# Small inputs by the GpSimd queue, a new order for the first two tiles, w_co in whole rows, and crossbar transposes for MLP tiles 1 to 3

## What is computed

```python
# sub-layer 1
u, bg, cg, h = jnp.split(xn @ w_in, [...], axis=-1)        # 512 columns each
y_pool = pool_mix(u_ext, ...)   # four groups: mean over the last 2, 4, 8, 16 rows - u, then 128x128 maps
y_conv = bg * conv3(cg * h)     # depthwise, causal, width 3
merged = concat(group_rmsnorm(y_pool, 4 groups), group_rmsnorm(y_conv, 8 groups))
x = x + rmsnorm(merged @ w_out, g_mix_post)
# sub-layer 2
x = x + rmsnorm(cross_attn(rmsnorm(x, g_x_pre), mem_k, mem_v, w_q, w_co), g_x_post)
# sub-layer 3
hid = jnp.square(jax.nn.relu(rmsnorm(x, g_ff_pre) @ w_up))  # 4096 columns
x = x + rmsnorm(hid @ w_down, g_ff_post)
```

## Time and profile before

| | |
|---|---|
| median of 3 runs | 883.66 us (882.21 to 885.01) |
| the profiled execution | 873.56 us |
| its span on the slowest core (7) | 872.0 us (cores: 859.7 to 872.0) |
| PE busy | 829.7 us, 95% |
| DVE, ACT, POOL busy | 390.7, 373.0, 102.5 us |
| chain that ended last | PE 83%, DMA 8%, DVE 3%, ACT 2%, POOL 2%, issue 2% |
| granted TensorE clock | 0.995 of full speed on core 7 |
| DMA | 100.31 MB moved, 115 GB/s over the span |

### The profile page before, as it was taken

The page is one execution under the profiler, slowest core; times in us unless marked ns, Lnnn a source line. Parts: engine busy times, 40 slices in busy tenths (PEclk is TensorE's granted clock), DMA queues, the critical chain, the costliest instruction groups (busy, mean ns, idle before and its releaser), DMA issues.

```text
span 872.0 us, 14089 instructions; the slowest of 8 cores (859.7 to 872.0 us)
## 1 busy us (share of the span) xinstructions
PE 829.7 (95%) x4818; PEld 404.9 (46%) x4818; DVE 390.7 (45%) x538; ACT 373.0 (43%) x806; POOL 102.5 (12%) x169
## 2 busy tenths in 40 slices
PE   2899999999998999999998999999999999999996
PEld 2444445554453455445454445444444444444442
DVE  4587767567865565668223213232222231322112
ACT  4557656657775565676332113340223311233101
POOL 4462102413210000100010000000000000000000
PEclk9999999999999999999999999999999999999999
DMA  8993076870069545794889724883139830185001
GB/s 206 220 167 52 18 234 168 159 109 1 2 88 161 108 153 174 130 166 94 146 144 166 174 97 103 144 151 93 49 112 159 152 85 25 49 146 96 17 33 49
DMA packets 31674, 100.31 MB, mean 115 GB/s; under 512 B 2666, under 2 KB 15978, under 8 KB 26356
## 3 DMA queue, kind: packets, MB, share of 16 engines
q0 software_dynamic: 20592, 65.15, 44.0%
q1 hardware_dynamic: 10436, 34.14, 11.6%
q10 hardware_dynamic: 576, 0.13, 0.1%
HBM read 142.28 MB, written 18.07 MB: 184 GB/s over the span
## 4 chain that ended last, share of the span: by engine, by line
PE 83%; DMA 8%; DVE 3%; ACT 2%; POOL 2%; issue 2%; SPq 0%; POOLq 0%; DVEq 0%; ACTq 0%
PE ps L639 80%; PE ps L644 3%; DMA wco<-w_co 3%; DMA wdn_131<-w_down 2%; DMA up_124<-w_up 1%; POOL sAB_94 L677 1%; DMA sT<-sconv 1%; DMA O_57<-mem 1%; POOL sAB_95 L677 1%; ACT xs_60 L668 0%; DVE xT_55 L675 0%; DVE X L688 0%; DVE O_57 L675 0%; ACT rf_101 L668 0%; DVE O_58 L675 0%
## 5 line engine op out<-in xcount | busy, mean ns | idle before, releaser
L675 DVE TENSOR_TENSOR O_57<-ps,gp 128x1024 f32<-128x1024 f32 x24 | 29.3, 1222 | 100.3 <-PE ps L639 74.3
L675 DVE TENSOR_TENSOR O_58<-ps,gp 128x1024 f32<-128x1024 f32 x24 | 29.3, 1222 | 98.2 <-PE ps L639 61.0
L668 ACT ACTIVATE rt_122<-ps 128x512 bf16<-128x512 f32 x64 | 38.2, 597 | 72.0 <-PE ps L639 69.7
L668 ACT ACTIVATE rt_121<-ps 128x512 bf16<-128x512 f32 x64 | 38.2, 596 | 71.8 <-PE ps L639 71.8
L668 ACT ACTIVATE O_58<-ps 128x1024 f32<-128x1024 f32 (+1 forms) x25 | 24.9, 996 | 98.7 <-PE ps L639 97.9
L668 ACT ACTIVATE O_57<-ps 128x1024 f32<-128x1024 f32 (+1 forms) x26 | 25.3, 972 | 97.6 <-PE ps L639 93.8
L639 PE MATMUL ps<-xT_55,win 128*128 128x512 bf16 x256 | 63.1, 392 | 1.3 <-DVE xT_55 L675 1.3
L639 PE MATMUL ps<-xT_56,win 128*128 128x512 bf16 x256 | 59.3, 379 | 0.1
L639 PE MATMUL ps<-xT_56,up_123 128*128 128x512 bf16 x192 | 42.4, 379 | 0.0
L639 PE MATMUL ps<-xT_55,up_124 128*128 128x512 bf16 x192 | 42.4, 379 | 0.0
L639 PEld LDWEIGHTS ps<-xT_55,win 128*128 128x128 bf16 x256 | 25.1, 100 | 31.1 <-issue 5.7
(11 more groups left out here) (302 smaller groups left out, 1504.2 us busy)
## 6 DMA issues: line engine op xcount, KB each, us to landing
up_123<-w_up POOLq DMA_DIRECT2D x11, 1024.0 KB, 9.2
up_124<-w_up POOLq DMA_DIRECT2D x11, 1024.0 KB, 10.4
up_125<-w_up POOLq DMA_DIRECT2D x10, 1024.0 KB, 10.2
x<-X SPq DMA_DIRECT2D x16, 512.0 KB, 4.0
X<-x SPq DMA_DIRECT2D x16, 512.0 KB, 4.3
yp<-X SPq DMA_DIRECT2D x16, 512.0 KB, 2.6
X<-xp SPq DMA_DIRECT2D x8, 512.0 KB, 6.5
win<-w_in POOLq DMA_DIRECT2D x4, 768.0 KB, 35.9
```

Of the source, the lines that this page charges most:

```text
L668: return e.activation(out=L(out), in_=L(in_), func=func, scale=scale, **kw)
L675: opts.append(("dve", lambda e, L: e.tensor_tensor(out=L(out), in0=L(in0), in1=L(in1), op=op), c_dve(n, per)))
```

## The change

Seven edits:

1. f4, Xs and sT are loaded from POOL's queue, sT first, and so are gp and gps of the first sub-layer.
2. Tile 1 is loaded by four loads of 512 KB behind w_in part 3, where one of 2 MB stood ahead of it.
3. The work of the first two tiles gets another order. Before: groups 0 to 3 of tile 0 and tile 1 interleaved, then the conv groups in pairs. After: the four pool groups of tile 0, the sample rows' states, conv groups 0 and 1 of tile 0 with the halves of tile 1's `pre_tile` behind them, the four pool groups of tile 1, its conv groups 0 and 1, and then conv groups 2 and 3 in pairs.
4. For tiles 0 and 1 the squares in `pre_sub` go to a spare buffer `junk` and no longer to xs. The scaling of rows may be done by DVE, ACT or POOL, as the planner finds, in every `pre_sub`.
5. w_co lies in memory as one row of 32 KB per partition, no longer as 16 blocks with 2 KB per partition, and is loaded with the planner's rate for large blocks.
6. For the MLP of tiles 1, 2 and 3 the transposes of xT are DMAs: `pre_tile_dma` squares and scales as before, then one `dma_start_transpose` on SP per sub-tile writes the 128x1024 block transposed into xT, and eight DVE operations apply the column gains in place.
7. For the last sub-tile of all, `post_halves` does square, multiply, add and store by halves of 512 columns.

The planner's cost for issuing a load from POOL changes as well.

```diff
-    wout_d = din("w_out", [128, 8192]); wco_d = din("w_co", [16, 128, 512])
+    wout_d = din("w_out", [128, 8192]); wco_d = din("w_co", [128, 8192])
+    junk = at("junk", A0 + 16384, D, BF16)
+    def scale_rows(out, in_, rs):
+        n = ncols(out)
+        P.add([("dve", lambda e, L: e.tensor_scalar(out=out, in0=in_, scalar1=rs, scalar2=None, op0=ALU.mult), c_dve(n, 0.5)),
+               ("act", lambda e, L: e.activation(out=out, in_=in_, func=AF.Copy, scale=rs), c_act(n)),
+               ("pool", lambda e, L: e.tensor_scalar(out=out, in0=in_, scalar1=rs, scalar2=None, op0=ALU.mult),
+                0.2 + n * 0.0009)], reads=[in_, rs], writes=[out])
-        return P.add([(q, lambda e, L: e.dma_start(out=out, in_=in_), 0.9 if q == "pool" else 0.43)],
+        return P.add([(q, lambda e, L: e.dma_start(out=out, in_=in_), 0.5 + nbytes / desc * 0.0005 if q == "pool" else 0.43)],
     def load_late():
-        load(f4[:, :], fold4[:, :], 65536)
-        load(Xs[:, :], xs4[:, :], 131072)
-        load(sT[0:32, :], spool[:, :], 65536)
-        load(sT[32:36, :], sconv[:, :], 8192)
+        load(sT[0:32, :], spool[:, :], 65536, q="pool")
+        load(sT[32:36, :], sconv[:, :], 8192, q="pool")
+        load(f4[:, :], fold4[:, :], 65536, q="pool")
+        load(Xs[:, :], xs4[:, :], 131072, q="pool")
-    def pre_sub(X, r, gc, dst):
+    def pre_sub(X, r, gc, dst, sq_out=None):
-        act(xs, X, AF.Square, accum=ss)
+        act(xs if sq_out is None else sq_out[0:r, :], X, AF.Square, accum=ss)
         rs = rstd(ss, r)
-        ts(xs, X, rs, ALU.mult)
+        scale_rows(xs, X, rs)
+    def post_halves(ps, X, gp, dst):
...
+        act(half(Ob, 0), ps.v(0, 128, 0, 512), AF.Square, accum=s0)
+        act(b0, s0, AF.Identity, scale=1.0 / D, bias=epsb[:, 0:1])
+        tt(half(Ob, 0), ps.v(0, 128, 0, 512), half(gp, 0), ALU.mult)
+        act(half(Ob, 1), ps.v(0, 128, 512, 1024), AF.Square, accum=s1)
+        tt(half(Ob, 1), ps.v(0, 128, 512, 1024), half(gp, 1), ALU.mult)
+        act(a, s1, AF.Ln, scale=1.0 / D, bias=b0)
+        act(rs, a, AF.Exp, scale=-0.5)
+        for h in range(2):
+            stt(half(X, h), half(Ob, h), rs, half(X, h), ALU.mult, ALU.add)
+            dma("sp", half(dst, h), half(X, h), 262144, wr=False)
+    def pre_tile_dma(t, gc, buf):
+        for i in range(NSUB):
...
+            act(xs, X, AF.Square, accum=ss)
+            rs = rstd(ss, 128)
+            scale_rows(xs, X, rs)
+            dst = r3(buf[:, :], 8)[:, :, i * 128:(i + 1) * 128]
+            P.add([("sp", lambda e, L, dst=dst, xs=xs: e.dma_start_transpose(out=dst, in_=xs), 0.43)],
+                  reads=[xs], writes=[dst], nbytes=262144)
+        for c in range(8):
+            v = buf[:, c * TN:(c + 1) * TN]
+            ts(v, v, gcs[:, gc * 8 + c:gc * 8 + c + 1], ALU.mult, per=0.25)
-    pre_tile(0, 0, xT[0])
-    second = load_four(1, xp, "pool")
-    for k in range(3, 7):
-        load_win(k)
+    pre_tile(0, 0, xT[0], junk)
+    load_win(3)
+    load_tile(1, xp, q="pool")
+    load_win(4)
+    load_win(5)
+    load_win(6)
...
-    load_gp("g_mix_post", second)
-    load_gps(0, second)
+    load_gp("g_mix_post", q="pool")
+    load_gps(0, q="pool")
     for g in range(4):
         step(pool_group(0, g))
-        if g == 1:
-            pre_tile(1, 0, xT[1])
-        if g >= 2:
-            step(pool_group(1, g - 2))
-    for g in range(2, 4):
+    ext_states()
+    ext_pool_rest()
+    ext_conv(0)
+    step(conv_group(0, 0))
+    pre_tile(1, 0, xT[1], junk, (0, 2))
+    ext_conv(1)
+    step(conv_group(0, 1))
+    pre_tile(1, 0, xT[1], junk, (2, 4))
+    for g in range(4):
         step(pool_group(1, g))
-    ext_pool_rest()
-    for cc in range(4):
+    for cc in range(2):
+        step(conv_group(1, cc))
+    for cc in range(2, 4):
         ext_conv(cc)
         step(conv_group(0, cc))
         step(conv_group(1, cc))
-            wload(wco[:, :], wco_d, 0, 16)
+            load(wco[:, :], wco_d[:, :], 4194304, q="pool", desc=16384)
-            pre_tile(t + 1, 2, xT[(t + 1) % 2])
+            pre_tile_dma(t + 1, 2, xT[(t + 1) % 2])
```

More of the change, by code:

```diff
@@ L795, in post @@
         return stt(X, Ob, rs, X, ALU.mult, ALU.add)
+    def post_halves(ps, X, gp, dst):
+        s0, b0, s1, a, rs = (stat(128) for _ in range(5))
+        Ob = Or[o_n[0] % 2]
+        o_n[0] += 1
+        half = lambda x, h: x[:, h * 512:(h + 1) * 512]
+        act(half(Ob, 0), ps.v(0, 128, 0, 512), AF.Square, accum=s0)
[8 more added lines that the diff above has]
+            dma("sp", half(dst, h), half(X, h), 262144, wr=False)
     x_n = [0]
@@ L808, in load_tile, with pre_tile, out_tile @@
         return ops
-    def load_four(t, src, q):
-        s = x_n[0] % 8
-        for i in range(NSUB):
[L813 to L821, removed]
-            dst = r3(buf[:, :], 8)[:, :, i * 128:(i + 1) * 128]
-            pre_sub(Xof[(t, i)], 128, gc, dst)
-    def out_tile(t, chunks, nk, w, gp, dst, hook=None):
+    def pre_tile(t, gc, buf, sq_out=None, part=(0, NSUB)):
+        for i in range(*part):
+            dst = r3(buf[:, :], 8)[:, :, i * 128:(i + 1) * 128]
+            pre_sub(Xof[(t, i)], 128, gc, dst, sq_out)
+    def pre_tile_dma(t, gc, buf):
+        for i in range(NSUB):
+            X = Xof[(t, i)]
+            ss = stat(128)
+            xs = xsr[xs_n[0] % 2][:, :]
+            xs_n[0] += 1
+            act(xs, X, AF.Square, accum=ss)
+            rs = rstd(ss, 128)
+            scale_rows(xs, X, rs)
+            dst = r3(buf[:, :], 8)[:, :, i * 128:(i + 1) * 128]
+            P.add([("sp", lambda e, L, dst=dst, xs=xs: e.dma_start_transpose(out=dst, in_=xs), 0.43)],
[3 more added lines that the diff above has]
+            ts(v, v, gcs[:, gc * 8 + c:gc * 8 + c + 1], ALU.mult, per=0.25)
+    def out_tile(t, chunks, nk, w, gp, dst):
         for i in range(NSUB):
@@ L832, in out_tile @@
             X = Xof[(t, i)]
-            last = post(ps, X, 128, gp)
-            if hook is not None:
-                hook(i, last)
+            row = t * TN + i * 128
+            if dst is yp and t == NT - 1 and i == NSUB - 1:
+                post_halves(ps, X, gp, yp[row:row + 128, :])
+                continue
+            post(ps, X, 128, gp)
             if dst is None:
                 continue
-            row = t * TN + i * 128
             dma("sp", dst[row:row + 128, :], X, 524288, wr=(dst is not yp))
@@ L849, in rstd_s, with load_gps @@
         return b
-    def load_gps(k, after=None):
-        load(gps[:, :], gs4[k], 131072, lead=LEAD // 2, after=after)
+    def load_gps(k, q="sp"):
+        load(gps[:, :], gs4[k], 131072, q=q, lead=LEAD if q == "pool" else LEAD // 2)
     def out_smp(chunks, nk, w):
@@ L1011, in ext_pool_proj, with ext_states @@
             copy(U[g][:, 0:16], ps.v(0, 128, NS, NX), eng="act")
-    def ext_pool_rest():
+    def ext_states():
         for g in range(4):
@@ L1018, in ext_pool_rest @@
             copy(vs(g)[:, :, 0:2], ps.v(0, 128, 32, 36, F32, lambda a: a.rearrange("p (b c) -> p b c", b=2)), eng="dve")
+    def ext_pool_rest():
         for g in range(4):
@@ L1258, in load_down, with load_gp @@
             load(dparts[k][:, :], wdn_d[k], 2097152, q="pool", after=after, desc=16384)
-    def load_gp(n, after=None):
-        load(gslot[n][:, :], gd[n][0:1, :].broadcast_to([128, D]), 524288, lead=LEAD // 2, after=after)
+    def load_gp(n, q="sp"):
+        load(gslot[n][:, :], gd[n][0:1, :].broadcast_to([128, D]), 524288, q=q, lead=LEAD if q == "pool" else LEAD // 2)
     load_tile(0, xp, q="pool")
@@ L1269, in build_program @@
     load_late()
-    pre_sub(Xe[0:NX, :], NX, 0, r3(xTe[:, :], 8))
-    pre_tile(0, 0, xT[0])
-    second = load_four(1, xp, "pool")
-    for k in range(3, 7):
-        load_win(k)
+    pre_sub(Xe[0:NX, :], NX, 0, r3(xTe[:, :], 8), junk)
+    pre_tile(0, 0, xT[0], junk)
[4 more added lines that the diff above has]
+    load_win(6)
     load(wout[:, :], wout_d[:, :], 4194304, q="pool", desc=16384)
-    load_gp("g_mix_post", second)
-    load_gps(0, second)
+    load_gp("g_mix_post", q="pool")
+    load_gps(0, q="pool")
     for k in range(2):
@@ L1451 @@
         "w_q": blk(chunks(f(w_q[0]).reshape(D, D), 128)),
-        "w_qT": blk(rows(f(w_q[0]).reshape(D, D).T)), "w_co": blk(rows(f(w_co[0]).reshape(D, D))),
+        "w_qT": blk(rows(f(w_q[0]).reshape(D, D).T)), "w_co": f(rows(f(w_co[0]).reshape(D, D))).reshape(128, -1),
         "w_up": oct(chunks(w_up[0], 128)), "w_down": oct(rows(w_down[0])),
```

## The result

The kernel after takes 924.85 us (median of 4 runs, 920.72 to 938.29) against 882.93 for the kernel before: a ratio of 1.0467, interval 1.0371 to 1.0563. The forecast was 869.9 us. The profiled execution is the longest of the four (938.29 us); in the other three too some cores end at 871 to 887 us and others above 915. The ratios of this document leave out executions in which a die's cores ran at a lower granted clock or that lie 1.5% above the kernel's fastest; medians in us do not, and of e1 only the two executions that remain are compared.

A forecast was written before the change was run, and what follows sets the result against it. PE bounds the MLP; loads feed the start to 76 us, and waits also lower the clock. Terms 4.0 + 0.5 + 4.5 + 3.6 - 0.4 + 1.4 = 13.6 us: 873.56 to 859.96, median 869.9; range 861 to 882.

The forecast's parts named there:

- I take 3, nearest to the store of the same size, and it is hidden: MLP: each transposing DMA takes 3 us, near a 256 KB store's 2.0, and holds nothing up.
- The upper bound of 19 us: MLP: a transposing DMA's highest estimated time, if each 256-byte row costs as much as an average load packet, 0.30 us.
- The third rival: MLP tile 1: transposing DMAs crowd out w_up at its first refill; at 12 us each, 888 us, median 898; chance 10%.
- Its break-even of 8.4 us each: MLP tile 1: the time per transposing DMA above which the whole change turns slower, 8.4 us.
- the gain of 3.6 - 0.4 = 3.2 us: MLP: dropping PE transposes gains 3.6 us at tiles 2 and 3; tile 1's longer w_down wait costs 0.4.
- `scale_rows` on ACT or POOL is paid from idle time after 76 us: Row scaling after 76 us: ACT or POOL does it in idle time, with no cost entered in the sum.
- the start, 4.0 us: Start, tile 0: first 512-column matmul at 20.1 us against 24.22, taken as a gain of 4.0 us.
- one of up to 4 us opens: Between the start and 76 us: a PE hole of up to 4 us opens, or one closes, about even.
- w_co, 4.5 us: w_co load: long rows land it 5.5 us sooner, shortening PE's wait and its clock loss; gain 4.5 us, between 0 and 5.7.
- 2.8 and a rest of 1.2 us: w_co: the planner may put the fold 2.8 us earlier on PE, leaving about 1.2 us of wait.
- it can't lose more than the few tenths: Tail, last sub-tile by halves: gain 1.4 us, at worst losing the few tenths of one more issue.
- the order of loads and tiles (+0.5): Between the start and 76 us: the new order gains 0.5 us, between +3.9 and -5.6.

The follow-up runs named there:

- e1: Kernel after with MLP tiles 1 to 3 transposed on PE again; 893.39 and 895.15 us in the two executions that remain.
- e2: Kernel after with row scaling on DVE or ACT only, never POOL, transposing DMAs kept; 919.43 us, 1.0407 of before.
- e6: Kernel before plus edit 6 alone, the planner told that xT is ready for the column gains 40 us later; 894.69 us, 1.0228 of before.
- e5: Kernel before plus edit 6 alone, each transposing DMA waiting for the last w_up load of its tile; 870.19 us, 0.9952 of before.
- e12: e5 plus the option of scaling rows on ACT or POOL at the planner prices of after; 883.14 us, 1.0082 of before.
- e15: e13 plus edits 1 and 4 without POOL scaling, order of loads and tiles as before; 868.60 us, 0.9904 of before.
- e13: e10 plus edit 7 with both adds ahead of both stores; 865.20 us, 0.9870 of before.
- e10: e5 plus the new layout of w_co alone, planner left at its old rate; 866.25 us, 0.9898 of before.
- e4: Kernel after with PE transposes again and no row scaling on POOL; 880.17 us, 1.0046 of before.
- e7: e4 with the order of loads and tiles of before (edits 2 and 3 undone); 878.43 us, 1.0030 of before.
- e16: e15 plus the new order of loads and tiles (edits 2 and 3); 870.26 us, 0.9911 of before.
- e17: Kernel before plus edit 6 alone, its twelve transposing DMAs replaced by plain ones in the same 256-byte packets, transposition left out; 886.58 us, 1.0101 of before.

## Why the prediction was wrong

- **Failed, and it decides: "I take 3, nearest to the store of the same size, and it is hidden"** (edit 6). Neither holds. The upper bound of 19 us was nearer, and itself too low: most transposes land in 3 to 6 us, those caught beside w_up take up to 34 in after and 42 in e2. Nor is it hidden: PE stops behind DVE's list (18.5 and 26.8 us on core 5 of after), and with that out of the way it waits for w_up (22.9 us on core 1 of e6). The third rival had the place (tile 1's last transposes at w_up's refill) and the kind of price, with a chance of 10%; it named only the second of these two paths. Its break-even of 8.4 us each was for all four; in fact one of tile 1's collapsed on some cores (two in e2), and tile 3's last as well. I took the price from a row in which nothing else was in flight. In quiet stretches the gain of 3.6 - 0.4 = 3.2 us was right: e5 gives 0.0048 x 876 = 4.2.
- **Failed: "`scale_rows` on ACT or POOL is paid from idle time after 76 us"** (edit 4). It costs 11.4 us (e12). Idle time of an engine did not pay for a scaling that takes 3.1 us in place of the planner's 1.12: PE waits for it, and for what stands in order behind it.
- **Failed: the start, 4.0 us.** The first matmul came near the forecast (21.06 for 20.1), but e15, with it, is no faster than e13 (3 us slower, the intervals just touch). The DMA share of 0.96 in the earlier trace rows said so: the loads set the pace up to 76 us. The bound "one of up to 4 us opens" came true on core 4 of e15 (a wait of 3.9), and should have been the value.
- **Half right: w_co, 4.5 us.** The layout gives it (e10: 0.0054 x 876 = 4.7). In the change PE waits for w_co as long as before (2.5 us on average in e4), because the planner moved the fold 4.4 us forward, where I reckoned 2.8 and a rest of 1.2 us (my own terms give 4.13 - 5.5 + 2.8 = 1.4).
- **Failed: the tail, "it can't lose more than the few tenths".** It lost 1.3 us to a wait that the tracker made: the store of one half is noted as a reader of the whole X, and the add of the other half waits for it. I counted operations and no dependencies. Without that wait the tail takes 6.6 us in e13 and 8.0 in e10: the 1.4 that I took.
- **Not shown either way:** the order of loads and tiles (+0.5). e4 and e7, and e15 and e16, can't be told apart.

Together, from run to run: 4 us (e4 against before), 32 (the transposing DMAs, e2 against e4) and 5 (POOL's scaling, after against e2) make 41, measured 42. In the other order POOL's scaling is 13 to 15 (e1 against e4) and the transposes 23 to 24.

## What to carry to other kernels

The price of a transfer taken from a quiet stretch holds for quiet stretches: ask what each DMA will run beside, and put transposing ones where no large load is due, by a dependency if need be (0.9952 in place of 1.0157 for one added wait). In a stretch whose DMA engines are full, an earlier start of the compute engine need not be a gain (e15). With a planner, look at what a changed cost moves, and give it the measured price of every option it may choose.

## What the runs showed of the hardware

- 256 KB transposed from SBUF to SBUF: 1024 packets of 256 bytes in some 1.5 us when alone (e5). The page "Advanced Engine Details and Errata" of the Trainium skill (X-Bar Transpose (TRN2)) calls transposing DMAs as fast as others; that holds there (plain copies of the same packets in e17: 1.3 to 1.5 us) and not beside 1 MB loads, where the landing took up to 34 us in after and 42 in e2, with 59 to 164 GB/s for everything together (plain copies 170 to 205). Not every meeting does it: in e6, core 0's fourth transpose passed in 2 us beside a w_up load (412.3 to 414.2). What tells the two apart stays open.
- SP is held some 1.23 us by a transposing DMA (after, core 5: 1.22 to 1.38, once 2.79), 0.6 by a plain one of the same packets (e17), and some 0.33 by most other plain ones (after, core 5).
- POOL scales 128x1024 f32 to bf16 in 3.1 us (after, core 5) to 3.2 us (e12, core 4); DVE takes 0.75 to 0.80, ACT 1.14 (after, core 5).
- Of cores 0 and 1, 2 and 3, 4 and 5, 6 and 7 one is often 7 to 15 us longer than the other, and which one changes between runs (e4: 861.8 and 877.0 for cores 0 and 1 in one run, 879.2 and 866.2 in another). PE's waits for w_co, w_v and w_down are 2 to 6 us longer in sum on the longer one (before and e4, all pairs); I did not try why.
